# Differential heads: scores from rounded parts and remainders, and the value chunk first in each group

## What is computed

```python
proj = jnp.einsum('bsd,dc->bsc', x, w_in[l])
q_a, k_a, v_a, q_b, k_b, v_b = jnp.split(proj, splits, axis=-1)
# heads 0-7: q_a, k_a as [B, S, 8, 2, 64]
s = jnp.einsum('bqhmd,bkhmd->bhmqk', qi, k) * scale      # causal
p = jax.nn.softmax(...)
a = p[:, :, 0] - lam * p[:, :, 1]
o = jnp.einsum('bhqk,bkhd->bqhd', a, v)
```

## Time and profile before

| | |
|---|---|
| runs, median | 1095.04 us |
| the profiled execution's own time | 1094.98 us |
| its span | 1093.2 us, 13845 instructions |
| TensorE busy | 1081.4 us, 99% |
| VectorE busy | 810.1 us, 74% |
| ScalarE busy | 568.4 us, 52% |
| GpSimd busy | 23.3 us, 2% |
| granted TensorE clock | 0.998 of full speed |
| HBM read | 210.83 MB, 195 GB/s over the span |

### The profile page before, as it was taken

One profiled execution on the slowest core, in us unless ns is written; L12 is line 12 of the kernel. 1 busy time (PEld: TensorE's weight loads), 2 busy tenths in 40 slices (PEclk: granted clock), 3 DMA queues, 4 the chain that ended last, 5 costly groups with the idle time before them and its releaser, 6 DMA issues.

```text
span 1093.2 us, 13845 instructions
## 1 busy us (share of the span) xinstructions
PE 1081.4 (99%) x5579; PEld 918.2 (84%) x5579; DVE 810.1 (74%) x893; ACT 568.4 (52%) x714; POOL 23.3 (2%) x45
## 2 busy tenths in 40 slices
PE   9999999999999999999999999999999999999996
PEld 8888888888888878888888888888888888888885
DVE  6587757666656685667699898666776678889998
ACT  6487757665544524445455454344454455554560
POOL 1000000010000000000000000000000000000001
PEclk9999999999999999999999999999999999999999
DMA  9857665557545834665656556466656655655852
GB/s 296 266 176 223 184 186 154 175 173 250 168 160 171 288 100 156 191 191 175 219 185 229 195 192 235 158 188 191 190 175 208 217 171 197 226 193 192 297 203 78
DMA packets 107903, 213.83 MB, mean 196 GB/s; under 512 B 6768, under 2 KB 37744, under 8 KB 107328
## 3 DMA queue, kind: packets, MB, share of 16 engines
q1 hardware_dynamic: 107216, 209.74, 59.4%
q0 software_dynamic: 624, 3.21, 1.0%
HBM read 210.83 MB, written 2.10 MB: 195 GB/s over the span
## 4 chain that ended last, share of the span: by engine, by line
PE 98%; DVE 1%; issue 0%; POOL 0%; ACT 0%; DVEq 0%
PE low_ps L780 11%; PE low_ps L619 10%; PE high_ps L780 10%; PE high_ps L800 8%; PE high_ps L798 8%; PE high_ps L799 8%; PE low_ps L512 6%; PE low_ps L516 6%; PE low_ps L514 6%; PE low_ps L785 5%; PE low_ps L624 5%; PE high_ps L785 5%; PE low_ps L800 2%; PE low_ps L798 2%; PE low_ps L799 2%; PE high_ps L559 1%
## 5 line engine op out<-in xcount | busy, mean ns | idle before, releaser
L1231 DVE TENSOR_TENSOR w_lo<-w_raw,w_hi 128x1024 fp32r<-128x1024 f32 x175 | 213.2, 1222 | 129.0 <-ACT w_hi L925 128.0
L925 ACT ACTIVATE w_hi<-w_raw 128x1024 fp32r<-128x1024 f32 x175 | 185.2, 1059 | 187.1 <-PE low_ps L516 66.9
L780 PE MATMUL low_ps<-x1T,w_hi 128*128 128x512 f32 x512 | 176.7, 393 | 0.0
L619 PE MATMUL low_ps<-xT,w_hi 128*128 128x512 f32 x448 | 156.8, 397 | 0.0
L780 PE MATMUL high_ps<-x1T,w_hi 128*128 128x512 f32 x448 | 155.0, 394 | 0.0
L785 PE MATMUL low_ps<-x1T,w_lo 128*128 128x256 f32 x512 | 136.9, 278 | 0.0
L1555 DVE TENSOR_TENSOR w_lo<-w_raw,w_hi 128x1024 fp32r<-128x1024 f32 x72 | 87.1, 1222 | 64.6 <-ACT w_hi L1124 64.6
L624 PE MATMUL low_ps<-xT,w_lo 128*128 128x256 f32 x448 | 122.3, 283 | 0.0
L1124 ACT ACTIVATE w_hi<-w_raw 128x1024 fp32r<-128x1024 f32 x72 | 76.1, 1059 | 88.8 <-PE low_ps L780 43.4
L785 PE MATMUL high_ps<-x1T,w_lo 128*128 128x256 f32 x448 | 119.8, 278 | 0.0
L798 PE MATMUL high_ps<-w_hi,hid 128*128 128x512 f32 x288 | 112.0, 389 | 0.0
(11 more groups left out here) (202 smaller groups left out, 1900.1 us busy)
## 6 DMA issues: line engine op xcount, KB each, us to landing
w_raw<-in_w_ff SPq DMA_DIRECT2D x208, 512.0 KB, 4.4
w_raw<-in_w_in SPq DMA_DIRECT2D x93, 512.0 KB, 4.1
more_raw<-in_w_ff SPq DMA_DIRECT2D x42, 512.0 KB, 5.3
w_raw<-in_w_out SPq DMA_DIRECT2D x32, 512.0 KB, 3.7
x_raw<-in_x_turned SPq DMA_DIRECT2D x8, 256.0 KB, 6.3
y<-in_x SPq DMA_DIRECT2D x8, 256.0 KB, 4.5
side_raw<-in_w_ff SPq DMA_DIRECT2D x4, 512.0 KB, 6.7
w_raw<-in_w_in SPq DMA_DIRECT2D x6, 256.0 KB, 5.2
```

The source lines that it names most:

```text
L619: return pe.matmul(banks[:, b, :], w_hi[:, slot, cols], xT[:, t, :, :].rearrange("p h t -> p (h t)"), start=(t == 0), stop=(t == KT - 1))
L780: return pe.matmul(banks[:, b, :], w_hi[:, slot, cols], x1T[:, t, :, :].rearrange("p h t -> p (h t)"), start=(t == 0), stop=(t == KT - 1))
L925: act.activation(w_hi[:, slot, :], w_raw[:, slot, :], ACT.Copy).then_inc(w_rounded, units)
L1231: dve.tensor_tensor(w_lo[:, slot, :], w_raw[:, slot, :], w_hi[:, slot, :].bitcast(F32), ALU.subtract).then_inc(w_split, units)
```

## The change

Scores of heads 0 to 7 are no longer fp32 products. Queries and keys after the rotary step are split into a rounded part and a remainder, both fp32r. For map m of a head the query tile `q_split[:, j, m, :]` holds the rounded queries in the 64 rows of the map and their remainder in the other 64 rows; `k_split[:, j, m, :]` holds the rounded keys twice, in both halves. One product over 128 rows gives high by high and low by high; a second one over the 64 rows of the map adds rounded queries by the remainder of the keys (`k_low`). The product of the two remainders is left out.

The split takes four new pieces of work for the 8 chunks of groups 0 and 1. Two steps after `ROPE_AFTER`, `round_qk` (ScalarE) makes two rounding copies of 64 rows by 512 columns, and `split_qk` (VectorE) two subtractions of that shape. Three steps after it, for chunks of keys, `double_k` (ScalarE) makes two more copies. VectorE's rotary sum goes to `qk_rot` first. `copy_low` waits for the rotary terms of the chunk before, and `rotate` for its split. Scores wait for `k_doubled` too. Heads 0 and 1 are scored after units 26 and 30.

The values come first in every group. The rotary chunks of group 1 end at units 35, 39, 43 and 47 (before: 27, 31, 35, 39), those of groups 2 and 3 four and eight units later than before in the same way: 59 to 71 (before 51 to 63), 83 to 95 (before 75 to 87). The values are copied at steps 14, 31, 55 and 79 (before 14, 47, 71, 95). `SCORE_AT` of heads 2 to 15 is unchanged.

```diff
--- before.py
+++ after.py
@@ -42,7 +42,8 @@
 OUT_END = [OUT_ORDER.index((n, UPH - 1)) + 1 for n in range(CHUNKS)]
 
 SCORE_AT = [24 * (h // 4) + 22 + (6 if h < HEADS - 4 else 3) * (h % 4) for h in range(HEADS)]
-SCORE_AT[0] += 2
+SCORE_AT[0] += 4
+SCORE_AT[1] += 2
 PROBS_AT = SCORE_AT[1:] + [SCORE_AT[-1] + 2]
 VALUES_AT = SCORE_AT[2:] + [SCORE_AT[-1] + 2, SCORE_AT[-1] + 4]
 OUTPUT_AT = [VALUES_AT[h] + 3 for h in range(N_DIFF)]
@@ -53,7 +54,7 @@
 IN_PLAN = []
 for group in range(GROUPS):
     pairs = [(which, group, half) for half in range(2) for which in range(2)]
-    IN_PLAN += [(2, group, 0)] + sorted(pairs) if group == 0 else pairs + [(2, group, 0)]
+    IN_PLAN += [(2, group, 0)] + (sorted(pairs) if group == 0 else pairs)
 IN_UNITS = [(c, k) for c, (which, group, half) in enumerate(IN_PLAN)
             for k in range(UPH if which == 2 else KT // KQ)]
 OPENING = 2 * UPH
@@ -65,6 +66,7 @@
 ROPE_CHUNK = [i for i, (which, group, half) in enumerate(IN_PLAN) if which < 2]
 VALUE_CHUNK = [i for i, (which, group, half) in enumerate(IN_PLAN) if which == 2]
 ROPE_AFTER = [CHUNK_END[i] + (2 if i == 2 else 0) for i in ROPE_CHUNK]
+SPLIT_AFTER = ROPE_AFTER[:4 * N_DIFF // PER_GROUP]
 VALUES_AFTER = [CHUNK_END[i] for i in VALUE_CHUNK]
 FF_PARTS = ((0, 7), (7, 16))
 FAST_CHUNKS = range(1, CHUNKS_FF - 1)
@@ -199,6 +201,9 @@
     scores = at("scores", [P, 2, KEYS], F32, A0 + 19 * KB)
     qT = at("qT", [P, 2, PER_GROUP, SEQ], F32, X0)
     kT = at("kT", [P, 2, PER_GROUP, SEQ], F32, X0 + 8 * KB)
+    q_split = at("q_split", [P, PER_GROUP, 2, SEQ], F32R, X0)
+    k_split = at("k_split", [P, PER_GROUP, 2, SEQ], F32R, X0 + 8 * KB)
+    k_low = at("k_low", [P, PER_GROUP, SEQ], F32R, X0 + 28 * KB)
     v_sb = [at(f"v_sb{n}", [P, TT, NC], F32, X0 + 16 * KB + n * 8 * KB) for n in range(2)]
     probs = at("probs", [P, 2, KEYS], F32, X0 + 20 * KB)
 
@@ -282,6 +287,7 @@
     turned, turn_rounded, turn_split = sem("turned"), sem("turn_rounded"), sem("turn_split")
     proj_done, v_copied = sem("proj_done"), sem("v_copied")
     rope_terms, roped = sem("rope_terms"), sem("roped")
+    qk_turned, qk_rounded, k_doubled = sem("qk_turned"), sem("qk_rounded"), sem("k_doubled")
     low_copied, qk_summed, rotated = sem("low_copied"), sem("qk_summed"), sem("rotated")
     scores_done, masked, max_found = sem("scores_done"), sem("masked"), sem("max_found")
     exp_done, sum_inverted = sem("exp_done"), sem("sum_inverted")
@@ -353,6 +359,14 @@
 
     def maps_of(h):
         return 2 if h < N_DIFF else 1
+
+    def rows_of(m):
+        return slice(m * HALF_DIM, (m + 1) * HALF_DIM)
+
+    def split_heads(r):
+
+        which, group, half = IN_PLAN[ROPE_CHUNK[r]]
+        return which, maps_of(PER_GROUP * group), slice(2 * half, 2 * half + 2)
 
     def in_chunk(i):
 
@@ -552,13 +566,22 @@
                 pe.wait_ge(ident_loaded, 16)
             g, j = h // PER_GROUP, h % PER_GROUP
             pe.wait_ge(roped, 4 * g + 2 * (j // 2) + 2 if h > 1 else 3)
-            width = P // maps_of(h)
-            for m in range(maps_of(h)):
-                rows = slice(m * width, (m + 1) * width)
+            if maps_of(h) == 1:
                 for tt in range(TT):
-                    ins = pe.matmul(scores_ps[:, m, keys_of(tt)],
-                                    qT[rows, g % 2, j, tt * P:(tt + 1) * P],
-                                    kT[rows, g % 2, j, 0:(tt + 1) * P], start=True, stop=True)
+                    ins = pe.matmul(scores_ps[:, 0, keys_of(tt)],
+                                    qT[:, g % 2, j, tt * P:(tt + 1) * P],
+                                    kT[:, g % 2, j, 0:(tt + 1) * P], start=True, stop=True)
+                ins.then_inc(scores_done, 1)
+                return
+            pe.wait_ge(k_doubled, 2 * g + j // 2 + 1)
+            for m in range(2):
+                rows = rows_of(m)
+                for tt in range(TT):
+                    toks, keys = slice(tt * P, (tt + 1) * P), slice(0, (tt + 1) * P)
+                    pe.matmul(scores_ps[:, m, keys_of(tt)], q_split[:, j, m, toks],
+                              k_split[:, j, m, keys], start=True, stop=False)
+                    ins = pe.matmul(scores_ps[:, m, keys_of(tt)], q_split[rows, j, m, toks],
+                                    k_low[rows, j, keys], start=False, stop=True)
             ins.then_inc(scores_done, 1)
 
         def turn_probs(h):
@@ -716,9 +739,9 @@
             def free(tt):
 
                 if n == 0:
+                    pe.wait_ge(qk_summed, 4 * GROUPS - 1)
+                elif n == 1:
                     pe.wait_ge(qk_summed, 4 * GROUPS)
-                elif n == 1:
-                    pe.wait_ge(v_copied, GROUPS)
                 else:
                     pe.wait_ge(y1_summed, TT * (n - 2) + tt + 1)
             if n < 2:
@@ -956,18 +979,38 @@
             i = ROPE_CHUNK[r]
             act.wait_ge(w_used, CHUNK_END[i] + 1)
             if r:
-                act.wait_ge(roped, r)
+                act.wait_ge(rope_terms, 2 * r)
             act.activation(qk_sum[:, :, :], in_banks(i)[:, :, SEQ:2 * SEQ], ACT.Copy).then_inc(
                 low_copied, 1)
 
         def rotate(r):
 
             act.wait_ge(qk_summed, r + 1)
+            if r:
+                act.wait_ge(roped, r)
             half = P // maps_of(PER_GROUP * (r // 4)) // 2
             for first in range(0, P, 2 * half):
                 for a, b in ((first, first + half), (first + half, first)):
                     ins = act.activation(qk_rot[a:a + half, :, :], qk_sum[b:b + half, :, :], ACT.Copy)
             ins.then_inc(rotated, 1)
+
+        def round_qk(r):
+
+            which, maps, heads = split_heads(r)
+            dst = (q_split, k_split)[which]
+            act.wait_ge(qk_turned, r + 1)
+            for m in range(2):
+                ins = act.activation(dst[rows_of(m), heads, m, :], qk_rot[rows_of(m), :, :], ACT.Copy)
+            ins.then_inc(qk_rounded, 1)
+
+        def double_k(r):
+
+            which, maps, heads = split_heads(r)
+            if which == 1 and maps == 2:
+                for m in range(2):
+                    ins = act.activation(k_split[rows_of(1 - m), heads, m, :], qk_rot[rows_of(m), :, :],
+                                         ACT.Copy)
+                ins.then_inc(k_doubled, 1)
 
         def exponentials(h):
             act.wait_ge(max_found, 2 * h + 2)
@@ -1013,6 +1056,10 @@
                 exponentials(SCORE_AT.index(n - 1))
 
         def attention_after(n):
+            if n - 2 in SPLIT_AFTER:
+                round_qk(SPLIT_AFTER.index(n - 2))
+            if n - 3 in SPLIT_AFTER:
+                double_k(SPLIT_AFTER.index(n - 3))
             if n in ROPE_AFTER:
                 copy_low(ROPE_AFTER.index(n))
             if n - 1 in ROPE_AFTER:
@@ -1266,9 +1313,24 @@
             dve.tensor_tensor(qk_rot[:, :, :], qk_rot[:, :, :], rope_table(r, 1),
                               ALU.mult).then_inc(rope_terms, 1)
             dve.wait_ge(rope_terms, 2 * r + 2)
-            which, group, half = IN_PLAN[ROPE_CHUNK[r]]
-            dst = (qT, kT)[which][:, group % 2, 2 * half:2 * half + 2, :]
-            dve.tensor_tensor(dst, qk_cos[:, :, :], qk_rot[:, :, :], ALU.add).then_inc(roped, 1)
+            if r >= len(SPLIT_AFTER):
+                which, maps, heads = split_heads(r)
+                dst = (qT, kT)[which][:, r // 4 % 2, heads, :]
+                dve.tensor_tensor(dst, qk_cos[:, :, :], qk_rot[:, :, :], ALU.add).then_inc(roped, 1)
+                return
+            dve.tensor_tensor(qk_rot[:, :, :], qk_cos[:, :, :], qk_rot[:, :, :],
+                              ALU.add).then_inc(qk_turned, 1)
+
+        def split_qk(r):
+
+            which, maps, heads = split_heads(r)
+            hi = (q_split, k_split)[which]
+            dve.wait_ge(qk_rounded, r + 1)
+            for m in range(2):
+                lo = (q_split[rows_of(1 - m), heads, m, :], k_low[rows_of(m), heads, :])[which]
+                ins = dve.tensor_tensor(lo, qk_rot[rows_of(m), :, :],
+                                        hi[rows_of(m), heads, m, :].bitcast(F32), ALU.subtract)
+            ins.then_inc(roped, 1)
 
         def mask_and_max(h):
             maps = maps_of(h)
@@ -1333,6 +1395,8 @@
                 combine(SCORE_AT.index(n - 1))
 
         def attention_after(n):
+            if n - 2 in SPLIT_AFTER:
+                split_qk(SPLIT_AFTER.index(n - 2))
             if n in ROPE_AFTER:
                 sum_qk(ROPE_AFTER.index(n))
             if n - 1 in ROPE_AFTER:
```

## The result

| | before | after |
|---|---|---|
| median | 1095.03 us (4 runs) | 1104.76 us (4 runs, 1104.55 to 1104.99) |
| profiled execution | 1094.98 us | 1104.6 us |
| span | 1093.2 us | 1102.8 us |

The account below looks back on a forecast made before the run. The prediction took TensorE, busy in 99% of the span, to bound the kernel. To the profiled 1094.98 us it added 9.6 for the score blocks and 0.4 for the opening: 1105.0 us, range 1098 to 1111.

Parts of the forecast that it names:

- TensorE's stream sets the time: Whole kernel: a microsecond added to or taken from TensorE's stream is one of the kernel's time; TensorE busy 99%.
- A change of row form costs 0.195 us, eight in place of two: Score blocks of heads 0 to 7: changes cost 1.56 us; with streams 2.27 against 1.06 a head, +9.6 us in all.
- The 128-column fp32r product at 0.06: Score blocks of heads 0 to 7: each such product takes 0.06 us, its lower bound by column rate; upper bound 0.22.
- the cheap rival: Rival on the score blocks: no change of row form is paid inside; 2.8 us less than before, 1092.2 us; chance 0.14.
- New work hidden: ScalarE's new copies and VectorE's subtractions cost nothing in the steady stretch; in the opening, narrowest cover is 0.7 us.
- The 0.4 us that I booked: Opening, splits of units 24 to 26: 0.4 us allowed because the estimated cover has an error of about one us.
- The order costs nothing: Values first, rotary chunks of groups 1 to 3 later by 4 to 8 units: 0 us; 2.8 us a unit if one fails.
- What would show it: Signs in the new profile: 7 gaps inside each block of heads 0 to 7, some 8 x 8 "issue" waits, block near 2.3 us.
- Units behind 26 have more room: Attention opening: argument against ScalarE and VectorE becoming the bound, that units after 26 have more cover; no size given.
- the bare load: Score blocks: case where each change of row form costs only the weight load, 0.105 us; 1.55 a block, 1098.9 us.
- the fp32 price: Rival on the score blocks: 128-column fp32r products take 0.22 us like fp32; 5.1 us more, 1110.1 us; chance 0.12.
- late weights: Rival in the opening: ScalarE and VectorE become the bound; 4.3 us in place of 0.4, 1108.9 us; chance 0.13.

Follow-up runs that it names:

- the padded kernel: The changed kernel with key remainders in a zero-padded tile per map, so second score products run over all 128 rows: 1095.07 us, ratio 0.9998.

## Why the prediction was right

- *TensorE's stream sets the time.* Right: 9.6 us more busy time, 9.7 us more in the median.
- *A change of row form costs 0.195 us, eight in place of two.* Right. The block came out at 2.27, the forecast to the hundredth, and 8 x 1.21 is 9.7. Three kernels with four, two and no changes show that the cost goes with the number of changes. The rule of the Trainium skill (TensorEngine Tiling (Array Packing), Key Properties) that a change of mode drains TensorE agrees with them. The fixed part of 166 ns (the Trainium skill, TensorE: Matmul & The Clock Gate, Single matmul latency), put on each change, would have been too dear: an estimate of 0.27 against the measured 0.195.
- *The 128-column fp32r product at 0.06.* Right where it stands between two changes (0.23 to 0.26 less 0.195). Where there is no change it costs 0.11, as much as a weight load. The term was right for this kernel and is not right in general; it is why the blocks of the padded kernel gain 1.0 us and not the 2.8 that the cheap rival reckoned with.
- *New work hidden.* Right. The copies took 0.63 and the two subtractions 1.39; ScalarE's work grew by 15.2 us, and twelve pairs of copies at 1.26 are 15.1. The splits of units 24, 25 and 26 ended at 71.87, 75.19 and 78.04 against 71.9, 75.2 and 77.9. Cover was 0.35 at the narrowest, not 0.7: unit 26 began 0.3 earlier than reckoned, half of it because units of values, which now stand there, are 2.72 us and not 2.8, and its split ended 0.14 later. The 0.4 us that I booked did not come. Without it the sum is 1104.6, and 1104.76 was measured. In the steady stretch from 103 to 141 us ScalarE was busy 28.5 and VectorE 27.5 of 38, not 33 and 32 of 40, since two chunks were split there and not three; the term was nothing either way.
- *The order costs nothing.* Shown by itself, with the old scores.
- *What would show it.* One sign was wrong. I expected weight loads waiting for "issue" some 64 times; the waits show one, of 0.2 us. The record of a load is 182 to 190 ns long and covers most of the 0.23 to 0.32 us between two starts. Only the distances between starts show the gaps.
- *Units behind 26 have more room.* Right for the changed kernel: the split of unit 30 ended at 90.62, 1.0 us before the unit began. It does not hold once the blocks get short: the cover of unit 30 was gone with four changes a head or fewer.

Two times of the rivals leave out the 0.4 us that the forecast had booked: with it, no change paid would be 1092.6 and the bare load 1099.3. Neither bears on the outcome. The rivals are excluded: the fp32 price by the block's rows (0.26 at most after a product of 128 columns, where it would be 0.22 + 0.195), late weights by the waits, and the cheap one by the block's rows and by the padded kernel, where the gaps go only with the changes.

## What to carry to other kernels

Before a product over part of the rows is put between products over all of them, count the changes of form, at about 0.2 us each here; grouping the products by form, or padding with zero rows, takes them away (2.27 to 1.09 and 0.93 us a block). A product that is cheaper by columns can be dearer by what stands around it, so price the sequence and not the instruction. When TensorE is made faster in an opening with little cover, look for the next late weight: here late weights took back 0.6 us, and scoring two heads one unit later gave it back.

## What was not expected of the hardware

Short fp32r products in a row cost what their weight loads cost: in the padded block the loads start 0.11 to 0.12 us apart, so that a product of 128 columns costs 0.11 us against 0.06 by columns. Two 64-row products of different maps, each adding into its own bank, run side by side in fp32r as in fp32: two take 0.26 us, with the change, as one does.
